# Splitting modulated rows into high and low bf16 parts: the shift taken off by GpSimd, the low part made by VectorE in one read of PSUM

## The chip, the cores and the metric

The kernel runs on one core of a Trainium2 chip. The metric is the device time of one execution in microseconds (us), smaller is better. All other times below are microseconds too, unless marked ns.

## The reference, cut to what matters

One layer of a hybrid diffusion backbone: a modulated RMSNorm feeds one combined projection (a gated convolution module and a bidirectional gated scan), an output projection follows, and then a routed mixture of 16 experts. The change is in the first part:

```python
sh1, sc1, ... = modulation(c, ada_w[l], ada_b[l])      # silu(c) @ ada_w + ada_b, split in 6
h_ctx = modulate(rmsnorm(ctx, norm1_g[l]), csh1, csc1) # h * (1 + scale) + shift
h     = modulate(rmsnorm(x, norm1_g[l]), sh1, sc1)
proj  = einsum('bnd,dc->bnc', h, w_in)                 # first use of h: columns A, B of the convolution
u     = conv(proj_A * sigmoid(proj_B), taps)
```

x has 2048 rows of 1024 channels and ctx has 256. Products of float32 operands are made from bf16 parts: each operand is a high part (its bf16 rounding) and a low part (the rest, in bf16), and three matmuls of parts stand for one product.

## The kernel before, in words

The program is a row of stages. Each stage is a block with one instruction stream per engine; all engines leave a stage before any enters the next. Two stages matter here.

**The front (`modulate_stage`, L96).** SP loads the conditioning vectors, four chunks of 512 columns of `ada_w` into `big`, then the rows: `xc` (group 0, 2 tiles of ctx), `xg1` (group 1, 4 tiles of x) and, over chunks that are used up, three more groups of 4 tiles. Two later chunks of `ada_w` (4 and 5) follow, and then the first four weight slabs of `w_in` into `wst`. TensorE multiplies each of the four chunks with the conditioning (L311, into `pm`), the result is copied (`mod_out`, L243), transposed into columns (L318) and copied again (`modc`, L263), and from it `A1` is made (L268): the factor of each channel. ScalarE squares rows for their mean squares (`square`, L207), VectorE inverts the roots (`inverse`, L248) and scales the rows (`normed`, L253).

Then comes the loop over q = 8g + k, that is 5 groups g by 8 blocks k of 128 channels, 40 steps. Called step q below:
- TensorE transposes the 2 or 4 tiles of block k into the PSUM bank `pt[q % 4]` (L331), and between the steps of the last three groups it runs the matmuls of chunks 4 and 5 (L339, two instructions each, and a bias pair, L342).
- ScalarE writes the high part `hhi` (bf16) from the bank, with factor and shift (L224); in groups 1 and 2 it also squares the rows of the group after next, from k = 4 on.
- VectorE reads the same bank again and writes the float32 value `hf` (L286); this sets the bank free for step q + 4. In groups 1 to 3 it also scales the rows of the next group, from k = 0 to 3.
- `hlo` = `hf` minus `hhi` is made by GpSimd for three steps of four and by VectorE for the fourth (L153).

VectorE copies the rows of chunks 4 and 5 out of PSUM behind groups 3 and 4 (L299); SP stores each to DRAM (L184) and waits for both stores before it leaves the stage.

**The convolution stage (`conv_stage`, L380).** ScalarE makes the high parts of weight slabs 0 to 3 (L526), VectorE their low parts (L613). TensorE takes blocks of 512 rows: each block needs two slabs (A and B columns) and 48 matmuls (L89 to L91), and there are four blocks for one pair of slabs. Block q + 2 waits until VectorE has made the gated product `u` of block q (L627). In VectorE's stream the first gated product stands behind two waits for parameters that GpSimd loads at the start of the stage: the convolution's taps and constants (L497 to L501, waited for at L618), and the gate's (L504 to L507, waited for at L621). VectorE's 124 convolution taps come next, while TensorE does the remaining blocks and other projections (jobs).

## Time and the profile before

| | us |
|---|---|
| median of 3 runs (2324.36 to 2325.8) | 2324.66 |
| the profiled execution | 2324.43 |
| its span, first to last instruction | 2322.3 |
| mean granted TensorE clock | 0.976 of full |
| end of the modulation (A1 made) | 50.95 |
| first compute of the convolution stage | 107.43 |
| its first matmul | 110.94 |

All times inside the execution count from the start of the span. The granted clock is 1.00 at 2.4 GHz and 0.50 at 1.2 GHz; a row between shows a stretch with both.

### The profile page before, as it was taken

To read this page: it belongs to the slowest core of one execution; us is meant where nothing else is said; L and a number is where in the kernel's file an instruction comes from. 1 tells how busy PE (TensorE), PEld (TensorE's weight loads), DVE (VectorE), ACT (ScalarE), POOL (GpSimd) and SP (SyncE) were. 2 spreads that over 40 slices of the span, in tenths; PEclk is the share of its full clock that TensorE was granted. 3 is DMA by queue.
4 is the path that set the end of the run, shared out by engine and by line. 5 is a ranking of instruction groups with operands and counts; after the bars stand their busy time and mean duration, and the time that the engine had idled before them with its cause. 6 is when DMAs were issued, how large, how long until landed. Compare 5 with 4: busy or idle time off the path is not lost. (4 is left out here: it accounts for less than half of the span.)

```text
span 2322.3 us, 38724 instructions
## 1 busy us (share of the span) xinstructions
PE 2188.7 (94%) x14885; PEld 1467.7 (63%) x14885; DVE 1607.5 (69%) x2235; ACT 1041.9 (45%) x1329; POOL 489.1 (21%) x535
## 2 busy tenths in 40 slices
PE   6799999999998898999976999999999999999995
PEld 3344444444878686755543777777777777777773
DVE  2839999784678787865566667666666666666666
ACT  3611002355566666644432444434444444443444
POOL 0610001012656565400003111011111111101111
PEclk9899999999999999999987999999999999999998
DMA  9341002455021120375444676676766766667776
GB/s 344 83 83 37 19 19 87 125 157 154 6 56 49 45 56 24 116 251 160 157 173 162 220 245 223 224 230 217 237 226 207 243 226 234 219 220 233 233 231 267
DMA packets 216932, 377.16 MB, mean 162 GB/s; under 512 B 38147, under 2 KB 79619, under 8 KB 216333
## 3 DMA queue, kind: packets, MB, share of 16 engines
q1 hardware_dynamic: 198702, 317.38, 40.6%
q0 software_dynamic: 16528, 56.47, 9.1%
q10 hardware_dynamic: 1616, 2.16, 0.3%
q8 instruction: 54, 0.88, 0.2%
q14 instruction: 32, 0.26, 0.0%
HBM read 313.44 MB, written 62.54 MB: 162 GB/s over the span
## 5 line engine op out<-in xcount | busy, mean ns | idle before, releaser
L89 PE MATMUL pgu<-xhi,mwhi 128*128 128x256 bf16 x2048 | 558.3, 273 | 0.0
L90 PE MATMUL pgu<-xlo,mwhi 128*128 128x256 bf16 x2048 | 558.3, 273 | 0.0
L91 PE MATMUL pgu<-xhi,mwlo 128*128 128x256 bf16 x2048 | 558.2, 273 | 0.0
L2416 DVE TENSOR_TENSOR mwlo<-mwst,mwhi 128x2048 bf16<-128x2048 f32 x187 | 426.8, 2282 | 0.0
L2313 ACT ACTIVATE mwhi<-mwst 128x2048 bf16<-128x2048 f32 x186 | 350.8, 1902 | 0.1
L2321 ACT ACTIVATE thb<-pgu 128x256 f32<-128x256 f32 x128 | 49.0, 383 | 547.2 <-PE pgu L91 547.2
L655 DVE SCALAR_TENSOR_TENSOR co<-u,taps,co 128x1984 f32<-128x1984 f32 (+22 forms) x120 | 234.1, 1951 | 3.7
L2427 DVE SCALAR_TENSOR_TENSOR thb<-thb,pgu 128x256 f32<-128x256 f32 x128 | 53.7, 420 | 258.3 <-ACT thb L2321 258.3
L90 PEld LDWEIGHTS pgu<-xlo,mwhi 128*128 128x128 bf16 x2048 | 200.4, 98 | 24.5
L89 PEld LDWEIGHTS pgu<-xhi,mwhi 128*128 128x128 bf16 x2048 | 200.4, 98 | 24.5
L2249 POOL TENSOR_TENSOR mpflag<-mpflag 1x1 f32<-1x1 f32 x46 | 37.5, 815 | 846.0 <-DVE ysb L2443 579.4
L91 PEld LDWEIGHTS pgu<-xhi,mwlo 128*128 128x128 bf16 x2048 | 200.4, 98 | 23.2
L2584 PE MATMUL pd<-mwhi,fhi 128*128 128x512 bf16 x512 | 194.1, 379 | 5.3 <-DVE ysb L2443 4.1
L2586 PE MATMUL pd<-mwhi,flo 128*128 128x512 bf16 x512 | 194.0, 379 | 0.0
L2585 PE MATMUL pd<-mwlo,fhi 128*128 128x512 bf16 x512 | 194.0, 379 | 0.0
L1497 PEld LDWEIGHTS pout<-E,KX 128*128 128x128 f32 (+2 forms) x1024 | 149.3, 180 | 43.6 <-issue 18.2
L1497 PE MATMUL pout<-E,KX 128*128 128x32 f32 (+2 forms) x1024 | 144.2, 233 | 21.0 <-DVE E L1314 12.8
L1474 PE MATMUL pj<-hhi,wst 128*128 128x512 bf16 (+1 forms) x320 | 108.3, 363 | 1.6 <-PEq L406 1.6
L2443 DVE SCALAR_TENSOR_TENSOR ysb<-pd,gate,g 128x512 f32<-128x512 f32 x64 | 47.9, 748 | 84.5 <-PE pd L2586 84.5
L1474 PE MATMUL pout<-hhi,wst 128*128 128x512 bf16 (+1 forms) x304 | 104.8, 373 | 0.0
L89 PE MATMUL pout<-hhi,whi 128*128 128x512 bf16 x256 | 97.0, 379 | 0.0
L90 PE MATMUL pout<-hlo,whi 128*128 128x512 bf16 x256 | 97.0, 379 | 0.0
(376 smaller groups left out, 4273.9 us busy)
## 6 DMA issues: line engine op xcount, KB each, us to landing
mwst<-in_w_gate SPq DMA_DIRECT2D x32, 2048.0 KB, 8.9
mwst<-in_w_up SPq DMA_DIRECT2D x32, 2048.0 KB, 7.9
mwst<-in_w_down SPq DMA_DIRECT2D x32, 2048.0 KB, 10.6
wst<-in_w_in SPq DMA_DIRECT2D x28, 512.0 KB, 6.1
big<-in_ada_w SPq DMA_DIRECT2D x5, 2048.0 KB, 14.0
s_rows<-row SPq DMA_DIRECT2D x16, 520.0 KB, 5.7
u<-in_ada_w SPq DMA_DIRECT2D x8, 1024.0 KB, 6.4
xt<-in_x SPq DMA_DIRECT2D x16, 512.0 KB, 4.3
```

Of the source, the lines that this page charges most:

```text
L89: nc.tensor.matmul(out, lh, rh, start=(first and k == 0), stop=False)
L90: nc.tensor.matmul(out, lh, rl, start=False, stop=False)
L91: ins = nc.tensor.matmul(out, ll, rh, start=False, stop=(last and k == n - 1))
L655: nc.vector.scalar_tensor_tensor(o, i, taps[:, c, k:k + 1], o, ALU.mult, ALU.add).then_inc(tap_ok, 1)
L1474: ins = nc.tensor.matmul(pj[i % 2][:, 0:n], w, x, start=(mm == 0), stop=(mm == 3 * KD - 1))
L1497: ins = nc.tensor.matmul(pat[0:keys, n * CH:(n + 1) * CH], KX[:, p, n * P:n * P + keys], E[:, p, n * CH:(n + 1) * CH], start=True, stop=True)
L2313: nc.scalar.activation(whi[:, b, ks], wst[:, b % NS, ks], ACT.Copy).then_inc(w_hi, 1)
L2416: nc.vector.tensor_tensor(wlo[:, b, ks], wst[:, b % NS, ks], whi[:, b, ks], ALU.subtract)\
L2427: nc.vector.scalar_tensor_tensor(thb[:, p], thb[:, p], 1.0, pgu[p][:, 0, :], ALU.add, ALU.mult)\
L2584: nc.tensor.matmul(pd[q % 2][:], fh, whi[:, 4 + c, k, :], start=(k == 0), stop=False)
L2585: nc.tensor.matmul(pd[q % 2][:], fh, wlo[:, 4 + c, k, :], start=False, stop=False)
L2586: last = nc.tensor.matmul(pd[q % 2][:], fl, whi[:, 4 + c, k, :], start=False, stop=(k == KD - 1))
```

## The change

The low part is taken another way. Before: hf = A1 * pt + shift, hlo = hf - hhi. Now GpSimd makes hms = hhi - shift, from SBUF alone, and VectorE makes hlo = A1 * pt - hms in one instruction, the only one in which it reads the bank. The bank becomes free with this instruction. Besides:

- The rows of group 1 are scaled ahead of the last copy of the modulation, the first two tiles of group 2 ahead of the `modc` copies, its other two tiles within group 0.
- The matmuls of chunks 4 and 5 go beside four of five of the first 20 steps of groups 2 to 4 (before: two of three of 24), and take the 128 columns of `cmix` as their stationary operand instead of the one column `sil`.
- The two copies at L299 move into groups 3 and 4 (behind k = 2 and k = 3).
- ScalarE and VectorE split weight slabs 0 and 1 within the last two groups of the front, into a buffer of their own (`wfirst`), in which the ctx rows stood before.

```diff
-        xc = m.sb("xc", [P, 2, D])
+        xc = CW_.first[:].rearrange("p a s k n -> p (a s k n)").bitcast(F32).rearrange("p (n d) -> p n d", d=D)
-        hf = m.sb("hf", [P, 4, SEG])
+        hms = m.sb("hms", [P, 4, SEG])
...
             def _(pool):
                 for q in range(NQ):
-                    if not on_dve(q):
-                        pool.wait_ge(hf_ok, q + 1)
-                        lo(nc.gpsimd, q)
+                    pool.wait_ge(hi_ok, q + 1)
+                    if q >= 4:
+                        pool.wait_ge(lo_ok, q - 3)
+                    nc.gpsimd.tensor_scalar(hms[:, q % 4, 0:width(q)], part(K["hhi"], q), shift(q), None, ALU.subtract)\
+                        .then_inc(hms_ok, 1)
...
             def _(act):
                         if k >= KD - 4 and 1 <= g < len(groups) - 2:
                             square(g + 2, k - (KD - 4))
+                        if g == len(groups) - 2 and k in (5, 7):
+                            w = (k - 5) // 2
+                            act.wait_ge(CW_.loaded[w], 16)
+                            CW_.high(nc, w, CW_.first[:, 0, w])
...
             def _(dve):
                 for n in range(NCH - 1):
                     mod_out(n)
-                inverse(0)
-                for j in range(groups[0][1]):
-                    normed(0, j)
+                for g in range(2):
+                    inverse(g)
+                    for j in range(groups[g][1]):
+                        normed(g, j)
                 mod_out(NCH - 1)
+                inverse(2)
+                normed(2, 0)
+                normed(2, 1)
                 for q in range(4):
                     dve.wait_ge(modc_ps, q + 1)
...
-                inverse(1)
-                for j in range(groups[1][1]):
-                    normed(1, j)
...
+                for g in range(len(groups)):
                     for k in range(KD):
                         q = g * KD + k
-                        dve.wait_ge(hi_ok, q + 1)
-                        if q >= 4:
-                            if on_dve(q):
-                                dve.wait_ge(lod_ok, q // 4)
-                            else:
-                                dve.wait_ge(lop_ok, pool_los(q - 4))
-                        nc.vector.tensor_scalar(hf[:, q % 4, 0:n * P], pt[q % 4][:, 0:n * P], A1[:, k, s:s + 1],
-                                                modc[:, k, s:s + 1], ALU.mult, ALU.add).then_inc(hf_ok, 1)
-                        if on_dve(q):
-                            dve.wait_ge(hf_ok, q + 1)
-                            lo(nc.vector, q)
-                        if k < 4 and 1 <= g < len(groups) - 1:
+                        dve.wait_ge(hms_ok, q + 1)
+                        nc.vector.scalar_tensor_tensor(part(K["hlo"], q), pt[q % 4][:, 0:width(q)], scale(q),
+                                                       hms[:, q % 4, 0:width(q)], ALU.mult, ALU.subtract).then_inc(lo_ok, 1)
+                        if g == 0 and k in (2, 5):
+                            normed(2, 2 + k // 5)
+                        if k < 4 and 2 <= g < len(groups) - 1:
                             if k == 0:
                                 inverse(g + 1)
                             normed(g + 1, k)
+                        if g == len(groups) - 1 and k in (0, 2):
+                            w = k // 2
+                            dve.wait_ge(CW_.hi_ok, w + 1)
+                            CW_.low(nc, w, CW_.first[:, 0, w], CW_.first[:, 1, w])
+                        if (g, k) in ((3, 2), (4, 3)):
+                            c = LATER[g - 3]
+                            dve.wait_ge(mod_ps, c + 1)
+                            dve.wait_ge(modc_ps, 4)
+                            nc.vector.tensor_copy(modrow[0:1, (c - 4) * SEG:(c - 3) * SEG], pm[c % 2][0:1, :]).then_inc(mod_sb, 1)
...
             def _(pe):
                         if q >= 4:
-                            pe.wait_ge(hf_ok, q - 3)
+                            pe.wait_ge(lo_ok, q - 3)
...
-                        if i >= 0 and i % 3 != 2:
-                            c, kk = LATER[(i - i // 3) // KD], (i - i // 3) % KD
+                        if 0 <= i < 20 and i % 5 != 4:
+                            c, kk = LATER[(i - i // 5) // KD], (i - i // 5) % KD
                             if kk == 0:
                                 pe.wait_ge(ada_in[c], 16)
-                            nc.tensor.matmul(pm[c % 2][0:1, :], K["sil"][:, kk:kk + 1], later(c)[:, kk, :], start=(kk == 0),
-                                             stop=False)
+                            nc.tensor.matmul(pm[c % 2][:], cmix[:, kk, :], later(c)[:, kk, :], start=(kk == 0), stop=False)
...
+        self.first = near.sb("wfirst", [P, 2, 2, KD, P], BF16)
+    def high(self, nc, s, out):
+        nc.scalar.activation(out, self.st[:, s % 4], ACT.Copy).then_inc(self.hi_ok, 1)
+
+    def low(self, nc, s, hi, out):
+        nc.vector.tensor_tensor(out, self.st[:, s % 4], hi, ALU.subtract).then_inc(self.lo_ok, 1)
...
-                for s in range(4):
+                for s in range(2, 4):
                     w_split(s)
```

The last hunk stands twice, in ScalarE's stream and in VectorE's. In the convolution stage slabs 0 and 1 are read from `wfirst`, and `whi` and `wlo` hold six slabs instead of eight.

## Rows read from the trace of the kernel before

**Rows 1.** The page: busy time by engine, and the chain that ended last by engine.
```profile
PE 2188.7 (94%) x14885; PEld 1467.7 (63%) x14885; DVE 1607.5 (69%) x2235; ACT 1041.9 (45%) x1329; POOL 489.1 (21%) x535
...
PE 43%; DVE 1%; issue 1%; ACT 0%; DMA 0%; POOL 0%; DVEq 0%; ACTq 0%; POOLq 0%
```

**Rows 2.** Windows: stretch, length, busy time (instructions) per engine, TensorE clock, DMA share, GB/s.
```profile
140.00:180.00 40.00, 40.00 (x187) 18.13 (x186) 23.60 (x16) 6.17 (x8) 0.76 (x1) 1.00 0.27 75
```

**Rows 3.** Who waited for whom, TensorE, 0 to 560: total, times, longest.
```profile
PE pa L89 <- DVE wlo L613: 8.7, 1, 8.7
PE pa L89 <- DVE u L627: 1.7, 1, 1.7
```

**Rows 4.** Timeline, VectorE, end of the modulation: start, length, engine, line, operation.
```profile
50.78 0.17 DVE L268 SCALAR_TENSOR_TENSOR A<-modc,n1c 128x16 f32<-128x16 f32 x1
...
51.20 2.74 DVE L253 TENSOR_SCALAR xg<-xg,rstd 128x1024 f32<-128x1024 f32 x4
53.86 1.90 DVE L286 TENSOR_SCALAR hf<-pt,A,modc 128x256 f32<-128x256 f32 x4
```

**Rows 5.** Groups by shape, whole execution: busy us, mean ns, idle before.
```profile
L1061 POOL TENSOR_SCALAR KK<-G,lh 128x512 f32<-128x512 f32 x32 | 23.6, 739 | 0.0
L2443 DVE SCALAR_TENSOR_TENSOR ysb<-pd,gate,g 128x512 f32<-128x512 f32 x64 | 47.9, 748 | 84.5 <-PE pd L2586 84.5
```

**Rows 6.** Groups by shape, 0 to 180.
```profile
L153 POOL TENSOR_TENSOR hlo<-hf,hhi 128x512 bf16<-128x512 f32 x24 | 31.6, 1340 | 12.7 <-DVE hf L286 12.6
...
L311 PEld LDWEIGHTS pm<-big,cmix 128*128 128x128 f32 x64 | 12.6, 203 | 30.1 <-issue 30.1
L613 DVE TENSOR_TENSOR wlo<-wst,whi 128x1024 bf16<-128x1024 f32 x10 | 11.8, 1219 | 3.8 <-ACT whi L526 3.8
```

**Rows 7.** Timeline, ScalarE: first step of group 1, first step of group 2.
```profile
58.41 4.19 ACT L224 ACTIVATE hhi<-pt,modc,A 128x512 bf16<-128x512 f32 x5 [1.31 <-PE pt L331]
...
69.10 0.78 ACT L224 ACTIVATE hhi<-pt,modc,A 128x512 bf16<-128x512 f32 x1
```

**Rows 8.** Timeline, TensorE, last steps of groups 2 and 4.
```profile
78.94 1.02 PE L339 MATMUL pm<-big,sil 128*1 128x512 f32 x2
...
95.61 0.66 PE L331 MATMUL pt<-ident,big 128*128 128x128 f32 x4
...
99.12 0.66 PE L331 MATMUL pt<-ident,big 128*128 128x128 f32 x4
...
101.60 0.66 PE L331 MATMUL pt<-ident,big 128*128 128x128 f32 x4
```

**Rows 9.** Timeline: VectorE's last of the front, the other engines' first after it.
```profile
104.56 0.67 DVE L299 COPY modrow<-pm 1x512 f32<-1x512 f32 x1
...
107.43 3.89 ACT L526 ACTIVATE whi<-wst 128x1024 bf16<-128x1024 f32 x4 [4.36 <-PEq L102]
...
110.94 0.61 PE L89 MATMUL pa<-hhi,whi 128*128 128x512 bf16 x1 [8.68 <-DVE wlo L613]
```

**Rows 10.** Timeline at the first stage boundary of the program.
```profile
2.13 0.29 POOL L2627 TENSOR_SCALAR_AFFINE_SELECT identb<-identb 128x128 bf16<-128x128 bf16 x1
2.73 1.28 ACT L199 ACT_TABLE_LOAD   x1 [2.73 <-PEq L2619]
```

**Rows 11.** Timeline, GpSimd, VectorE and TensorE around the first gated product.
```profile
127.02 0.78 POOL L499 DMA_DIRECT2D cb<-in_conv_bias  x1 [12.12 <-issue]
...
135.51 0.68 DVE L627 SCALAR_TENSOR_TENSOR u<-th,pa 128x512 f32<-128x512 f32 x1
...
136.25 0.39 PE L89 MATMUL pa<-hhi,whi 128*128 128x512 bf16 x1 [1.73 <-DVE u L627]
```

**Rows 12.** Windows: stretch, length, busy per engine, TensorE clock.
```profile
56.00:58.00 2.00, 1.21 (x7) 0.83 (x6) 2.00 (x5) 1.10 (x3) 1.19 (x3) 0.50 0.39 143
...
106.00:107.00 1.00, 0.00 (x0) 0.00 (x0) 0.00 (x0) 0.00 (x0) 0.00 (x0) 0.58 0.00 0
...
116.00:117.00 1.00, 1.00 (x5) 0.45 (x4) 0.00 (x0) 0.00 (x0) 0.00 (x0) 0.80 1.49 95
```

**Rows 13.** One line, all instructions of the one-input GpSimd form: ns min/median/max.
```profile
L1061 POOL TENSOR_SCALAR KK<-G,lh x40: 467/681/1607, 563.6 to 961.3; 128x512 f32<-128x512 f32 x32, 128x256 f32<-128x256 f32 x8
```

More of the change, by code:

```diff
@@ L142, in later, with part, width, shift @@
             return xg1[:].rearrange("p n d -> p (n d)").rearrange("p (k e) -> p k e", e=SEG)
-        def on_dve(q):
-            return q % 4 == 3
-        def pool_los(q):
-            return 3 * (q // 4) + min(3, q % 4 + 1)
-        def lo(engine, q):
+        def part(t, q):
             g, k = divmod(q, KD)
             t0, n = groups[g]
-            engine.tensor_tensor(K["hlo"][:, k, t0 * P:(t0 + n) * P], hf[:, q % 4, 0:n * P],
-                                 K["hhi"][:, k, t0 * P:(t0 + n) * P], ALU.subtract)\
-                .then_inc(lod_ok if on_dve(q) else lop_ok, 1)
+            return t[:, k, t0 * P:(t0 + n) * P]
+        def width(q):
+            return groups[q // KD][1] * P
+        def shift(q):
+            return modc[:, q % KD, 0:1] if q >= KD else modc[:, q % KD, 1:2]
+        def scale(q):
+            return A1[:, q % KD, 0:1] if q >= KD else A1[:, q % KD, 1:2]
         with nc.Block() as block:
@@ L218, in _ @@
                 act.wait_ge(a1_ok, 1)
-                for g, (t0, n) in enumerate(groups):
-                    s = 0 if g else 1
+                for g in range(len(groups)):
                     for k in range(KD):
@@ L223, in _ @@
                         act.wait_ge(tp_ps, q + 1)
-                        nc.scalar.activation(K["hhi"][:, k, t0 * P:(t0 + n) * P], pt[q % 4][:, 0:n * P], ACT.Identity,
-                                             bias=modc[:, k, s:s + 1], scale=A1[:, k, s:s + 1]).then_inc(hi_ok, 1)
+                        nc.scalar.activation(part(K["hhi"], q), pt[q % 4][:, 0:width(q)], ACT.Identity, bias=shift(q),
+                                             scale=scale(q)).then_inc(hi_ok, 1)
                         if k >= KD - 4 and 1 <= g < len(groups) - 2:
                             square(g + 2, k - (KD - 4))
+                        if g == len(groups) - 2 and k in (5, 7):
+                            w = (k - 5) // 2
+                            act.wait_ge(CW_.loaded[w], 16)
+                            CW_.high(nc, w, CW_.first[:, 0, w])
             @block.vector
@@ L446, in conv_stage, with high, low @@
         LATE = range(JOBS - 3, JOBS)
+        def high(w):
+            return CW_.first[:, 0, w] if w < 2 else whi[:, w - 2]
+        def low(w):
+            return CW_.first[:, 1, w] if w < 2 else wlo[:, w - 2]
         def to_store(j):
@@ L612, in w_split @@
                     w = SLAB[s][1]
-                    nc.vector.tensor_tensor(wlo[:, w], wst[:, s % 4], whi[:, w], ALU.subtract).then_inc(w_lo, 1)
-                for s in range(4):
+                    CW_.low(nc, s, high(w), low(w))
+                for s in range(2, 4):
                     w_split(s)
@@ L723, in _, with low_rows @@
                         square_sum(n + 1)
-                    def low(q):
+                    def low_rows(q):
                         dve.wait_ge(mh_ok, q + 1)
@@ L768, in job @@
                         last = triple(nc, bank[:], [
-                            (whi[:, w, k, :], wlo[:, w, k, :], K["hhi"][:, k, t0:t0 + SEG], K["hlo"][:, k, t0:t0 + SEG])
+                            (high(w)[:, k, :], low(w)[:, k, :], K["hhi"][:, k, t0:t0 + SEG], K["hlo"][:, k, t0:t0 + SEG])
                             for k in range(KD)])
@@ L781, in _ @@
                             last = triple(nc, bank[q % 2][:], [
-                                (whi[:, s, k, :], wlo[:, s, k, :], K["hhi"][:, k, t0:t0 + SEG],
+                                (high(s)[:, k, :], low(s)[:, k, :], K["hhi"][:, k, t0:t0 + SEG],
                                  K["hlo"][:, k, t0:t0 + SEG]) for k in range(KD)])
```

37 lines of the change are left out of this document (16 added, 21 removed).

## The prediction

> **What bounds the kernel now.** I read the page first. TensorE is busy 94% of the span, and of the chain that ended last TensorE is by far the largest engine [rows 1]. So what counts is where TensorE stands still. The windows show it without a gap from 140 on, at full clock, to about 540 [rows 2]: whatever comes earlier at about 136 comes earlier at the end, one to one. The list of its waits gives two places between the front and there: 8.7 us before the first matmul of the convolution stage and 1.7 us before its third block [rows 3]. The profiled execution took 2324.43, its span is 2322.3; 2.1 us lie around it. It stands 0.2 under the median, so a gain worked out in it is taken off 2324.66.
>
> **The modulation.** TensorE's first matmuls end with the fourth chunk, and A1 stands at 50.95. Then VectorE scales group 1 (2.74) and only at 53.86 reads the first bank [rows 4]: some 2.9 us in which four banks are full. The change moves these four scalings ahead, under the modulation's matmuls, where VectorE has nothing to do. Two scalings of group 2 (0.69 each, a quarter of 2.74) and a reciprocal stand ahead of the four modc copies. They end near 50.1 and the copies then run one behind the other, so A1 comes between 0 and 0.3 later: about 51.1.
>
> **Prices of the step.** GpSimd's new instruction, one SBUF input, 512 columns, is in the trace with float32 input: 739 ns [rows 5]. The same form ran from 467 ns (256 columns) to 1607 ns, median 681 [rows 13], and the two-input form that it replaces took 1340 [rows 6]. I take 0.74 and keep 0.68 to 1.6. The Trainium skill says of GpSimd (GPSIMD Engine Reference, Engine selection) that a two-input operation is about twice as slow as on VectorE while one input runs near line rate: the two rows agree. It also says (Advanced Engine Details and Errata, VectorE Performance Modes) that GpSimd and VectorE instructions in a two-port mode block each other; the scalings would be such, and by that rule the price moves up within groups 0, 2 and 3, which is a rival below. VectorE's new instruction reads a bank and an SBUF tile with a factor per partition; the nearest row is 748 ns [rows 5], about 0.70 from start to start. It replaces 5 instructions in four steps by 4. ScalarE is unchanged.
>
> **Length of one step's chain.** The bank is now held through transposes (0.53), high part (0.77), GpSimd (0.74), VectorE (0.70) and three hand-overs (about 0.1 each): 3.0, and 3.6 with TensorE at half clock. With four banks that allows a step every 0.76 to 0.9 us. Nothing in groups 1 to 4 is that quick, so the longer hold costs nothing as long as GpSimd keeps its price.
>
> **Groups 0 and 1.** In group 0 (256 columns) a round of four takes about 2.1, plus one scaling: the first bank is free at 53.2, step 8's at 55.7. TensorE at half clock, as the row of 56 to 58 has it now [rows 12], needs 0.85 for the transposes, so ScalarE starts group 1 at 56.6 instead of 58.41. Its work in group 1 (eight high parts, four squares, a root) took 10.7 [rows 7] and is not changed: group 2 starts on ScalarE at 67.1 instead of 69.10, a gain of 2.
>
> **Group 2.** The first low part ends 67.1 + 0.77 + 0.74 + 0.70 + 0.2 = 69.5. For four steps VectorE does a low part and a scaling, 1.4 each, and the transposes of steps 20 to 23 wait for these: 69.6, 71.0, 72.5, 74.0, with a matmul pair (0.95) behind each but the first. The group ends on TensorE at 75.5; it ended at 79.9 [rows 8].
>
> **Groups 3 and 4.** Now TensorE sets the pace. Three steps with two pairs took 95.61 to 99.12 [rows 8], which is 3 x 0.53 + 2 x 0.95. Group 3 has 8 steps, 6 pairs and a bias pair: 10.9, to 86.4. In group 4 are 3 steps, 3 pairs and a bias pair: 5.4, to 91.8. All pairs are done then; the rest is the chain of the last steps on VectorE. Low part 34 ends at 92.4, then come slab 1's low part (1.14; 1219 ns long [rows 6]), low part 35 (0.7), the copy (0.6), low parts 36 to 38 and, behind the wait for its transposes, 39: end at 98.2. It was 105.2 [rows 9]. The pairs now load 128 columns of weights, 203 ns each [rows 6]. These loads can lie under the transposes or stand in front of the pair; bounds are 0 and 0.2 for each of 16. I take 0.06, 1.0 in all.
>
> **The boundary.** Now the stage ends with the store of chunk 5's row: from the end of VectorE's copy at 105.23 to ScalarE's first at 107.43 are 2.2 us [rows 9]. The copy will end at 95.3, its store is back by 97.6, ahead of the last low part. A boundary without a store takes 0.3 [rows 10]. So the convolution stage starts at 98.2 + 0.3 + 1.0 = 99.5, against 107.4: **7.9 us earlier**.
>
> **The two slabs.** Before, TensorE began at 110.94, 3.5 behind the start of the stage [rows 9]. With slabs 0 and 1 ready it can begin 0.3 behind it. Their splitting costs ScalarE 2.1 in group 3 and VectorE 2.3 in group 4; the first lies under TensorE's pairs, the second is in the sum above. But the 3.2 us aren't kept. Block 2 waits for the first gated product, which stands in VectorE's stream behind GpSimd's parameter loads: GpSimd issues the next load only at 127.02 after 12.12 us, and the product starts at 135.51, TensorE at 136.25 [rows 11], 28.8 behind the start of the stage. The change leaves this chain alone. The two first blocks took 110.94 to 134.5. They will end some 24 behind the stage's start, and TensorE will wait about 5 instead of 1.73.
>
> **What the wait does to the clock.** At 106 to 107 the granted clock fell from 1.00 to 0.50, four microseconds after the last transposes (101.60), and it came back between 116 and 117, 5.4 us after matmuls had begun again [rows 8, 9, 12]. At half clock for 5.4 us TensorE loses 2.7. The wait of 1.73 left the clock alone; one of 5 is longer than those four. So I take a fall at block 2: **2.6 us lost**, and behind it TensorE has no gap in which to make it good. The Trainium skill has the same rule (TensorE: Matmul & The Clock Gate, Part 1): an array left idle returns to 1.2 GHz.
>
> **Sum.** 7.9 - 2.6 = 5.3 earlier: 2324.66 - 5.3 = 2319.4. What a measurement can tell from no change is 0.2%, 4.6 us, so faster means under 2320.0: the forecast is only just there.
>
> **Rivals.**
> - No fall of the clock at block 2 (the blocks end later than I think, or 5 us isn't enough): 7.9 earlier, 2316.8. For it: the row shows only that four idle microseconds preceded a fall. Chance 0.17.
> - The parameter chain gets shorter, and part of the slabs' 3.2 us is kept. The two slab splittings no longer run on VectorE while GpSimd writes its descriptors. Against it: most of the chain is the 12.12 us in which GpSimd does nothing visible. 8 to 11 earlier, down to 2313.7. Chance 0.10.
> - GpSimd costs 1.34, as the old form: the scalings hold it up. Then it sets the pace: 32 steps and 8 of half width, 36 x 1.34 = 48, from 52.0 to 100.2; with the last low part and the boundary the stage starts at 101.5 to 102. Gain 5.6 - 2.6 = 3: 2321.7. Chance 0.16.
> - Slower: GpSimd at the slowest seen, 1.607, in every step: 36 x 1.607 = 57.9, to 109.9, the stage starts at 111.1, 3.7 later, and the clock's 2.6 comes on top: 2331. From 1.44 us per step on (stage start 104.8) the change loses. The one row for it is a maximum of 40, whose median is 681. Chance 0.06.
> - The change does nothing to the end, since VectorE's taps bound the convolution stage and not TensorE. Against it: both start from the same first block, and TensorE has no idle time there [rows 2]. 2324.7. Chance 0.05.
>
> The forecast itself has 0.46, with a range of its own from 2317 to 2321.5: 0 to 3.2 for the weight loads, 1 for group 0's rounds, 1.7 to 3.4 for the clock. Two thirds of it lie under 2320.0. Faster: 0.31 + 0.17 + 0.10 = 0.58. Within 0.2%: 0.15 + 0.16 + 0.05 = 0.36. Slower: 0.06. The range from 2314.5 to 2322.5 leaves out the slower case, the null case and the far end of the shorter chain.
>
> **What would show it.** GpSimd's new line near 740 ns. ScalarE's first step of group 2 near 67. TensorE without waits in group 3. ScalarE's or TensorE's first of the convolution stage near 99.5, TensorE within 0.5 of the stage's start. A wait of about 5 before the third block, for the gated product, and a granted clock of 0.50 behind it. Wrong: a GpSimd line above 1.2, or banks for which TensorE waits in groups 3 and 4; the parameter chain at another length than 28.8; the clock at 1.00 at the third block.

## The result, and the profile after

The changed kernel took 2332.93 (median of 7; 2330.6 to 2334.78) against 2325.17 (2324.36 to 2326.4) for the kernel before: **0.3% slower**, ratio 1.0032 with the interval 1.0021 to 1.0044. It was run again later on another chip: 2332.38, ratio 1.0031 (1.002 to 1.0042). The forecast was 2319.4. The profiled execution took 2331.6, its span is 2328.7.

The groups by shape of the changed kernel, 0 to 180, GpSimd and then VectorE:

```profile
L195 POOL TENSOR_SCALAR hms<-hhi,modc 128x512 f32<-128x512 bf16 x32 | 52.9, 1674 | 0.0
L195 POOL TENSOR_SCALAR hms<-hhi,modc 128x256 f32<-128x256 bf16 x8 | 8.2, 1044 | 47.5 <-ACT hhi L225 47.5
...
L285 DVE SCALAR_TENSOR_TENSOR hlo<-pt,A,hms 128x512 bf16<-128x512 f32 x32 | 23.9, 748 | 19.6 <-POOL hms L195 19.6
```

The new GpSimd line costs 1674 ns, where the prediction took 740 from [rows 5]; VectorE's new line costs the 748 that was taken. The 19.6 of VectorE's idle time name the new bound. The timeline of GpSimd shows it in one row: 40 instructions from 51.90 on, 61.07 long, and no idle time inside.

```profile
51.90 61.07 POOL L195 TENSOR_SCALAR hms<-hhi,modc 128x256 f32<-128x256 bf16 x40 [47.52 <-ACT hhi L225]
115.13 7.09 POOL L511 DMA_DIRECT2D taps<-in_conv_taps  x4 [2.16 <-POOLq L102]
133.79 0.78 POOL L513 DMA_DIRECT2D cb<-in_conv_bias  x1 [11.57 <-issue]
```

Consecutive low parts on VectorE then stand 1.54 apart, each behind GpSimd:

```profile
97.07 0.75 DVE L285 SCALAR_TENSOR_TENSOR hlo<-pt,A,hms 128x512 bf16<-128x512 f32 x1 [0.79 <-POOL hms L195]
98.61 0.75 DVE L285 SCALAR_TENSOR_TENSOR hlo<-pt,A,hms 128x512 bf16<-128x512 f32 x1 [0.79 <-POOL hms L195]
...
113.01 0.75 DVE L285 SCALAR_TENSOR_TENSOR hlo<-pt,A,hms 128x512 bf16<-128x512 f32 x1 [0.79 <-POOL hms L195]
```

So a full step costs 1.54 from start to start where nothing lengthens it. 32 of these and 8 of 0.93 (half width) are 56.7; the other 4.4 of the 61.07 come in where VectorE works from SBUF beside it: ten scalings (two in group 0, four each in groups 2 and 3) and the low parts of the two early slabs, beside each of which a GpSimd instruction took 1.83. GpSimd's single instructions, and VectorE's scalings in the same stretch:

```profile
73.94 1.57 POOL L195 TENSOR_SCALAR hms<-hhi,modc 128x512 f32<-128x512 bf16 x1
75.48 2.35 POOL L195 TENSOR_SCALAR hms<-hhi,modc 128x512 f32<-128x512 bf16 x1
77.81 1.93 POOL L195 TENSOR_SCALAR hms<-hhi,modc 128x512 f32<-128x512 bf16 x1
```

```profile
74.87 1.18 DVE L258 TENSOR_SCALAR big<-big,rstd 128x1024 f32<-128x1024 f32 x1
...
76.63 0.74 DVE L258 TENSOR_SCALAR big<-big,rstd 128x1024 f32<-128x1024 f32 x1
...
78.54 0.74 DVE L258 TENSOR_SCALAR big<-big,rstd 128x1024 f32<-128x1024 f32 x1
```

The instruction of 77.81 has one scaling beside it and is 0.37 longer than the one of 73.94; that of 75.48 meets two and is 0.78 longer; the scaling at 74.87 is itself longer by 0.44. So the two engines do hold each other up, by 0.37 to 0.44 each time, about half of a scaling's 0.74, but the 1.54 is there without it.

The windows (length, busy time and instructions of PE, PEld, DVE, ACT and POOL, clock, DMA share, GB/s) show who sets the pace now. After, and below it the kernel before:

```profile
90.00:100.00 10.00, 7.41 (x34) 3.76 (x34) 6.78 (x10) 5.90 (x8) 10.00 (x6) 1.00 0.00 0
```

```profile
90.00:100.00 10.00, 9.29 (x43) 3.72 (x43) 9.93 (x15) 5.41 (x8) 7.61 (x7) 1.00 0.00 0
```

Before, TensorE and VectorE were both nearly full and GpSimd had a quarter of its time free. After, GpSimd is full and both others wait for it.

What came of that downstream, in the rows that answer to [rows 3] (TensorE's waits, 0 to 620) and [rows 9, 11] (timelines at the boundary and at the third block):

```profile
PE pt L333 <- DVE hlo L285: 14.6, 22, 1.7
...
PE pa L89 <- DVE u L641: 5.0, 1, 5.0
```

```profile
114.70 2.00 ACT L362 ACTIVATE whi<-wst 128x1024 bf16<-128x1024 f32 x2 [5.13 <-PEq L102]
115.10 0.63 PE L90 MATMUL pa<-hlo,wfirst 128*128 128x512 bf16 x1 [6.34 <-PEq L102]
...
142.28 0.68 DVE L641 SCALAR_TENSOR_TENSOR u<-th,pa 128x512 f32<-128x512 f32 x1
...
143.01 0.61 PE L89 MATMUL pa<-hhi,wfirst 128*128 128x512 bf16 x1 [4.97 <-DVE u L641]
```

The convolution stage starts at 114.70, 7.3 later than before. TensorE is with it at once, as the early slabs promise, but the third block starts 28.3 behind the stage's start (28.8 before), behind a wait of 4.97. And the clock falls in that wait:

```profile
140.00:142.00 2.00, 0.00 (x0) 0.00 (x0) 0.00 (x0) 0.00 (x0) 0.34 (x1) 0.54 0.29 2
142.00:144.00 2.00, 0.99 (x3) 0.43 (x4) 1.88 (x4) 0.00 (x0) 0.00 (x0) 0.50 0.00 0
```

The last matmul before the wait ends at 138.04; the clock falls at about 140.2 (0.54 is the mean of 140 to 142), 2.1 later. Matmuls run at 1.2 GHz from 143.01 to about 147, which costs 2. The next stage is the place to read the sum off, since TensorE has no other gap in between. Its first matmul, first before and then after:

```profile
559.82 0.27 PE L1474 MATMUL pj<-hhi,wst 128*128 128x256 bf16 x1 [1.60 <-PEq L406]
```

```profile
568.53 0.27 PE L1488 MATMUL pj<-hhi,wst 128*128 128x256 bf16 x1 [1.59 <-PEq L414]
```

That is 8.7 later: 6.8 at the third block (143.01 - 136.25) and 2 for the clock. The median moved by 7.8.

### The profile page after: what moved, and what is told of

The parts are those of the page before. It is cut to its first block and busy times, and to the rows that moved or that the text cites. A ratio compares the mean times of both kernels' runs of the same rounds, so it can differ in the third digit from the quotient of the medians.

```text
span 2328.7 us, 38579 instructions
## 1 busy us (share of the span) xinstructions
PE 2182.8 (94%) x14740; PEld 1472.0 (63%) x14885; DVE 1598.0 (69%) x2225; ACT 1042.7 (45%) x1329; POOL 516.5 (22%) x545
## 5 line engine op out<-in xcount | busy, mean ns | idle before, releaser
L2599 PE MATMUL pd<-mwlo,fhi 128*128 128x512 bf16 x497 | 188.4, 379 | 2.9 <-DVE flo L2449 1.4
L2598 PE MATMUL pd<-mwhi,fhi 128*128 128x512 bf16 x481 | 182.3, 379 | 4.2 <-DVE ysb L2457 4.1
L1488 PE MATMUL pj<-hhi,wst 128*128 128x512 bf16 (+1 forms) x306 | 101.8, 357 | 1.6 <-PEq L414 1.6
L1300 DVE TENSOR_TENSOR_SCAN B<-segm,E 128x512 f32<-128x512 f32 (+1 forms) x40 | 57.4, 1436 | 57.1 <-ACT E L1147 57.1
L549 ACT ACTIVATE jb<-pout 128x512 f32<-128x512 f32 (+1 forms) x54 | 31.5, 592 | 137.0 <-PE pout L91 119.3
```

Of the source, the lines that this page charges most:

```text
L1300: nc.vector.tensor_tensor_scan(B[:, p, way], segm[:, 0:n], E[:, p, way], 0.0, ALU.mult, ALU.add)\
L1488: ins = nc.tensor.matmul(pj[i % 2][:, 0:n], w, x, start=(mm == 0), stop=(mm == 3 * KD - 1))
L2598: nc.tensor.matmul(pd[q % 2][:], fh, whi[:, 4 + c, k, :], start=(k == 0), stop=False)
L2599: nc.tensor.matmul(pd[q % 2][:], fh, wlo[:, 4 + c, k, :], start=False, stop=False)
```

## The experiments

Each of the kernels with a time ran beside the kernel before on its chip, and the ratio is against that: the median of the kernel before was 2324.0 on the chip of "two operations", "old low part" and "no early slabs", 2325.22 on that of "before + 128 columns", "add and multiply" and the parameters on GpSimd, 2325.21 on that of the last two. The two kernels with trial instructions ran once each (2331.11 and 2332.41) and are read for the prices alone. All diffs are against the changed kernel unless said otherwise. "Next stage" is the start of TensorE's first matmul of the stage behind the convolution; "wait" is TensorE's wait before the third block, and "clock" the granted clock behind it.

| kernel | stage start | third block, wait | clock | next stage | median | ratio (interval) |
|---|---|---|---|---|---|---|
| before | 107.43 | 136.25, 1.7 | 1.00 | 559.82 | 2325.17 | |
| the change | 114.70 | 143.01, 5.0 | 0.50 | 568.53 | 2332.93 | 1.0032 (1.0021 to 1.0044) |
| two operations | 127.63 | 156.75, 6.4 | 0.50 | 582.91 | 2345.3 | 1.0095 (1.008 to 1.0111) |
| old low part | 103.82 | 132.46, 5.4 | 0.50 | 557.74 | 2321.46 | 0.9994 (0.9985 to 1.0003) |
| no early slabs | 115.18 | 143.97, 3.0 | 1.00 | 567.53 | 2331.42 | 1.0036 (1.0022 to 1.0049) |
| before + 128 columns | 106.71 | 135.73, 3.0 | 1.00 | 559.32 | 2321.73 | 0.999 (0.998 to 0.9999) |
| add and multiply | 99.56 | 128.94, 7.0 | 0.50 | 554.64 | 2322.47 | 0.9983 (0.9973 to 0.9992) |
| + parameters in the front, GpSimd | 113.48 | none | 1.00 | 559.88 | 2322.79 | 0.9989 (0.9979 to 0.9998) |
| + parameters in the front, SP | 99.24 | none | 1.00 | 545.17 | 2312.84 | 0.9942 (0.9928 to 0.9955) |
| the same, no early slabs | 102.21 | none | 1.00 | 552.94 | 2314.14 | 0.995 (0.9936 to 0.9963) |

### What makes GpSimd's instruction dear

Eight forms are tried three times each at the start of the front, where VectorE does next to nothing; the rest of the kernel is the changed one.

```diff
+                for _ in range(3):
+                    done(nc.gpsimd.tensor_scalar(o, b, col, None, ALU.subtract))
...
+                    done(nc.gpsimd.tensor_scalar(o, f, col, None, ALU.subtract))
+                    done(nc.gpsimd.tensor_scalar(o, b, 0.0, col, ALU.add, ALU.subtract))
+                    done(nc.gpsimd.tensor_scalar(o, f, -1.0, col, ALU.add, ALU.mult))
+                    done(nc.gpsimd.tensor_scalar(o, b, -1.0, col, ALU.add, ALU.mult))
+                    done(nc.gpsimd.tensor_scalar(o, b, col, None, ALU.add))
+                    done(nc.gpsimd.tensor_scalar(o, b, 1.0, None, ALU.mult))
+                    done(nc.gpsimd.tensor_tensor(o, b, f, ALU.subtract))
```

Each stands in a loop of three, as the first; b is bf16, f float32, col one value per partition. The lines are L205, L207 and so on to L219 in this order.

> The changed kernel with 24 instructions put into GpSimd's idle time at the start (some 47 us), three of each form, 512 columns, one after the other with a wait: they change nothing of the output. It prices the forms alone. The new instruction cost 1.54 to 1.56 us where 0.74 was expected. Theory A (the form with one operation and a per-partition operand is slow): bf16 and float32 input both near 1.5, the two-operation form near 0.74 with either input. Theory B (the bf16 input is slow): bf16 near 1.5 in all forms, float32 near 0.74 in all. Theory C (VectorE's scalings and bank reads hold GpSimd up): all forms near 0.74 here, where VectorE does next to nothing.

GpSimd's groups by shape, 0 to 52:

```profile
L209 POOL TENSOR_SCALAR hms<-hlo,eps 128x512 f32<-128x512 bf16 x3 | 6.0, 2005 | 0.3
L205 POOL TENSOR_SCALAR hms<-hlo,eps 128x512 f32<-128x512 bf16 x3 | 5.0, 1657 | 0.3
L207 POOL TENSOR_SCALAR hms<-hms,eps 128x512 f32<-128x512 f32 x3 | 4.7, 1567 | 0.3
...
L217 POOL TENSOR_SCALAR hms<-hlo 128x512 f32<-128x512 bf16 x3 | 4.5, 1498 | 0.3
L219 POOL TENSOR_TENSOR hms<-hlo,hms 128x512 f32<-128x512 bf16 x3 | 3.5, 1163 | 0.2
L211 POOL TENSOR_SCALAR hms<-hms,eps 128x512 f32<-128x512 f32 x3 | 2.1, 695 | 0.3
L213 POOL TENSOR_SCALAR hms<-hlo,eps 128x512 f32<-128x512 bf16 x3 | 2.1, 694 | 0.3
```

The mean of 1657 for the form of the change holds one instruction of 1836 ns (its line alone, ns min/median/max):

```profile
L205 POOL TENSOR_SCALAR hms<-hlo,eps x3: 1566/1570/1836, 5.5 to 9.1; 128x512 f32<-128x512 bf16 x3
```

It is the first, from 5.50 on, and VectorE still makes `cmix` beside it until 6.87. The other two take 1.57, the price in the kernel, with no VectorE work beside them: contention between the two engines is ruled out as the cause of the price. bf16 and float32 cost the same, in the subtraction (1.57 undisturbed, and 1567) as in the pair (694, 695): the type is ruled out too. L213 reads the same tile as L205 and costs less than half. What is left is the operations. The row of [rows 5] from which the price came (L1061) adds -1.0 and multiplies by a column; the change's instruction has one operation. A single operation is the dear case, even a multiplication by 1.0 (1498); so is add with subtract (2005), which the first theory had near 0.74.

A second set in the same place, L205 to L217 in this order, sorts the pairs.

```diff
+                    done(nc.gpsimd.tensor_scalar(o, b, col, 1.0, ALU.subtract, ALU.mult))
+                    done(nc.gpsimd.tensor_scalar(o, b, col, 1.0, ALU.add, ALU.mult))
+                    done(nc.gpsimd.tensor_scalar(o, b, 1.0, col, ALU.mult, ALU.add))
+                    done(nc.gpsimd.tensor_scalar(o, b, 1.0, col, ALU.mult, ALU.subtract))
+                    done(nc.gpsimd.tensor_scalar(o, b, 0.0, col, ALU.add, ALU.add))
+                    done(nc.gpsimd.tensor_scalar(o, b, 1.0, col, ALU.subtract, ALU.mult))
+                    done(nc.gpsimd.tensor_scalar(o, b, 0.0, 1.0, ALU.add, ALU.mult))
```

> The changed kernel with 24 more trial instructions in GpSimd's idle time at the start, three of each form, 512 columns. The first trials gave 0.69 us for add-then-multiply and 1.5 to 2.0 for a single operation or add-then-subtract, whatever the input's type. Theory A2 (a form whose second operation is a multiply is quick): subtract-then-multiply, add-then-multiply with the per-partition operand first, and both with immediates near 0.7; multiply-then-add, multiply-then-subtract and add-then-add near 2.0. Theory A3 (only add-then-multiply is quick): subtract-then-multiply near 2.0 too. Theory A4 (the per-partition operand must come second): only the last two-immediate form may be quick. A two-input subtraction of a broadcast column near 1.16 in all theories.

```profile
L205 POOL TENSOR_SCALAR hms<-hlo,eps 128x512 f32<-128x512 bf16 x3 | 6.0, 2013 | 0.3
L213 POOL TENSOR_SCALAR hms<-hlo,eps 128x512 f32<-128x512 bf16 x3 | 6.0, 2003 | 0.3
...
L209 POOL TENSOR_SCALAR hms<-hlo,eps 128x512 f32<-128x512 bf16 x3 | 2.1, 698 | 0.3
L207 POOL TENSOR_SCALAR hms<-hlo,eps 128x512 f32<-128x512 bf16 x3 | 2.1, 695 | 0.3
L217 POOL TENSOR_SCALAR hms<-hlo 128x512 f32<-128x512 bf16 x3 | 1.9, 620 | 0.3
```

Add with multiply is quick in either order (695, 698), with two immediates too (620). Each pair with a subtraction, and add with add, costs 2.0. None of the three theories came out: subtract-then-multiply is dear, against the first; multiply-then-add is quick, against the second; and the column may come first or second, against the third. A subtraction of a column in the quick form is therefore an addition of its negative.

### The price in the kernel

First the pair that turned out not to be quick, in the kernel itself:

```diff
-                    nc.gpsimd.tensor_scalar(hms[:, q % 4, 0:width(q)], part(K["hhi"], q), shift(q), None, ALU.subtract)\
+                    nc.gpsimd.tensor_scalar(hms[:, q % 4, 0:width(q)], part(K["hhi"], q), 0.0, shift(q), ALU.add, ALU.subtract)\
```

> The changed kernel with GpSimd's instruction written with two operations, add 0.0 and then subtract the shift: the same result in the form of the 0.74 us row. Theory A (form): GpSimd's instruction near 0.74, the front ends some 14 us earlier than in the changed kernel, TensorE sets the pace of groups 3 and 4, and the time is about 2319 (my forecast for the change). Theories B and C: no difference from the changed kernel, about 2333.

The instruction's median is 1997 ns, the stage starts at 127.63, and the time is 2345.3. A second operation as such is no help. The run tells something else: from the change to this kernel the stage's start moved by 12.9, the next stage by 14.4 and the median by 12.4. The front's end goes into the time about one to one, moved by the price of this one instruction.

Then the quick pair, with the negative of the shift in a column of its own:

```diff
+                nc.vector.tensor_scalar(lessc[:], modc[:, 0:KD, :], -1.0, None, ALU.mult).then_inc(less_ok, 1)
...
-                    nc.gpsimd.tensor_scalar(hms[:, q % 4, 0:width(q)], part(K["hhi"], q), shift(q), None, ALU.subtract)\
+                    nc.gpsimd.tensor_scalar(hms[:, q % 4, 0:width(q)], part(K["hhi"], q), less(q), 1.0, ALU.add, ALU.mult)\
```

> The changed kernel with GpSimd's instruction written as add minus-shift, then multiply by 1.0 (one more small VectorE instruction makes the column of minus shifts): the same result. If this form costs 0.7, the front is what my forecast took: convolution stage from about 98 to 100, wait of about 5 at the third block, time 2317 to 2319. If it costs 1.5 to 2.0, the time is that of the changed kernel or more.

```profile
L201 POOL TENSOR_SCALAR hms<-hhi,lessc 128x512 f32<-128x512 bf16 x32 | 24.6, 774 | 16.0 <-ACT hhi L231 15.7 <-DVE hlo L292 0.2
```

```profile
99.56 2.00 ACT L369 ACTIVATE whi<-wst 128x1024 bf16<-128x1024 f32 x2 [2.61 <-PEq L102]
...
128.94 0.61 PE L89 MATMUL pa<-hhi,wfirst 128*128 128x512 bf16 x1 [7.00 <-DVE u L648]
```

```profile
130.00:132.00 2.00, 2.00 (x6) 0.70 (x5) 1.75 (x3) 0.00 (x0) 0.00 (x0) 0.50 0.34 94
```

The mean of 774 holds instructions that were lengthened; the median of the line is 691 ns. The stage starts at 99.56; the prediction had 99.5. TensorE starts 0.02 behind it. The wait before the third block and the fall of the clock are there, and the next stage starts at 554.64, 5.2 earlier than before; the prediction had 5.3. The median is 2322.47, 2.75 under that of the kernel before on its chip, and the interval of the ratio spans 1.9 to 6.3 less: it is clear of none, and 5.2 lies inside it. The expected 2317 to 2319 was met by the profiled execution (2318.09), not by the median (see the last section).

### The other parts alone

The old low part (VectorE makes hf, GpSimd and VectorE subtract) with all else of the change:

```diff
-                    pool.wait_ge(hi_ok, q + 1)
...
+                    if not on_dve(q):
+                        pool.wait_ge(hf_ok, q + 1)
+                        lo(nc.gpsimd, q)
...
-                        nc.vector.scalar_tensor_tensor(part(K["hlo"], q), pt[q % 4][:, 0:width(q)], scale(q),
-                                                       hms[:, q % 4, 0:width(q)], ALU.mult, ALU.subtract).then_inc(lo_ok, 1)
+                        nc.vector.tensor_scalar(hms[:, q % 4, 0:width(q)], pt[q % 4][:, 0:width(q)], scale(q), shift(q),
+                                                ALU.mult, ALU.add).then_inc(hf_ok, 1)
```

> The changed kernel with the low part made as before (VectorE reads the bank into float32, GpSimd three of four subtractions, VectorE the fourth); scalings, matmul placing and the two early slabs stay changed. If GpSimd's instruction alone makes the change slow, the front's last low part comes at 99 to 101 instead of 113.8 and the time falls to 2318 to 2322. If the other parts share the blame, it stays above 2325.

The last low part ends at 102.78 (99 to 101 expected) and the stage starts at 103.82: the moved scalings, copies, matmuls and slabs are worth 3.6 there, and the new low part at its quick price another 4.3 (to 99.56). The median of 2321.46 lies in the expected range, but by the ratio the gain cannot be told from none (0.9994, 0.9985 to 1.0003). In the trace the third block is 3.8 earlier and the next stage 2.1: the slabs' 3 are lost in the wait of 5.4, and the clock behind it takes back 1.7.

The change without the early slabs:

```diff
-                        if g == len(groups) - 2 and k in (5, 7):
-                            w = (k - 5) // 2
-                            act.wait_ge(CW_.loaded[w], 16)
-                            CW_.high(nc, w, CW_.first[:, 0, w])
...
-                for s in range(2, 4):
+                for s in range(4):
```

> The changed kernel with slabs 0 and 1 split in the convolution stage as before. My theory: the third block waits for the parameter loads anyway, so the early slabs buy only a longer wait (5.0 instead of 1.7 us) and a fall of the clock behind it: without them the clock stays at 1.00 at the third block and the time is 2 to 3 us less than the changed kernel's, about 2330. Rival: the clock or the wait doesn't matter and the early slabs are worth up to 3 us: 2333 to 2336.

```profile
118.69 0.61 PE L89 MATMUL pa<-hhi,wfirst 128*128 128x512 bf16 x1 [9.44 <-DVE wfirst L357]
```

```profile
142.00:144.00 2.00, 0.03 (x1) 0.03 (x2) 0.92 (x4) 0.55 (x1) 0.00 (x0) 1.00 0.11 1
144.00:146.00 2.00, 2.00 (x10) 0.94 (x11) 2.00 (x3) 0.00 (x0) 0.00 (x0) 1.00 0.00 0
```

TensorE starts 3.6 later (118.69 for 115.10) and yet meets the next stage 1.0 earlier (567.53 for 568.53). Its wait before the third block is 3.0 in place of 5.0, and the clock stays at 1.00. Here the early slabs bring the third block 1.0 forward (143.01 for 143.97), half of it an earlier stage start, and cost 2 through the clock. That the clock stays at 1.00 was expected; the 2 to 3 of time were not seen: the medians (2331.42, 2332.93) do not tell the two apart.

The 128 columns alone, against the kernel before:

```diff
-                            nc.tensor.matmul(pm[c % 2][0:1, :], K["sil"][:, kk:kk + 1], later(c)[:, kk, :], start=(kk == 0),
+                            nc.tensor.matmul(pm[c % 2][:], cmix[:, kk, :], later(c)[:, kk, :], start=(kk == 0),
...
-                                nc.tensor.matmul(pm[c % 2][0:1, :], K["ones"][0:1, 0:1], adab2[0:1, c - 4, :], start=False,
+                                nc.tensor.matmul(pm[c % 2][:], K["ones"][0:1, :], adab2[0:1, c - 4, :], start=False,
```

The bias pair takes 128 columns too, as in the changed kernel.

> The kernel before with one edit: the matmuls of chunks 4 and 5 take the 128 columns of cmix as their stationary operand. In the changed kernel a step of transposes with a pair took 1.30 us where it was free to run, before 1.53. Theory: the one-column operand costs the time, so here steps with a pair come every 1.30 instead of 1.53 in groups 2 to 4, up to 16 x 0.24 = 3.8 us less in the front where TensorE sets the pace, some 2 of them in the end. Rival: the pitch comes from the order of the work and not from the operand; pitch and time stay (2324).

```profile
95.09 0.60 PE L331 MATMUL pt<-ident,big 128*128 128x128 f32 x4
95.52 1.02 PE L339 MATMUL pm<-xg,cmix 128*128 128x512 f32 x2
96.38 1.15 PE L331 MATMUL pt<-ident,big 128*128 128x128 f32 x8
```

And the kernel before:

```profile
74.84 0.66 PE L331 MATMUL pt<-ident,big 128*128 128x128 f32 x4
75.43 1.02 PE L339 MATMUL pm<-big,sil 128*1 128x512 f32 x2
76.38 1.09 PE L331 MATMUL pt<-ident,big 128*128 128x128 f32 x8
```

A step of four transposes and a pair takes 1.29 with 128 columns (95.09 to 96.38) and 1.54 with one (74.84 to 76.38). So the 128 columns do not cost up to 0.2 a pair, they save 0.25: the theory's pitch came true, and the rival's did not. But at the stage's start 0.7 is left of it, and at the next stage 0.5, not the expected 2. The interval of the ratio ends just under 1; the median is 3.5 lower than that of the kernel before, more than the 0.5 accounts for (see the last section).

### Taking the parameter chain out of the way

With the quick pair, the stage's start is won and the third block waits 7.0 for the parameters. Two kernels load them in the front, both with the edit of the quick pair. In the first GpSimd issues them:

```diff
+                pool.wait_ge(ada_in[0], 16)
+                CP_.load(nc, pool, I, GW_)
+                pool.wait_ge(less_ok, 1)
                 for q in range(NQ):
```

> As e7, and the loads of the convolution's taps and constants and of the gate's parameters issued by GpSimd in the front, behind the first chunk of ada_w, when it has nothing else to do. My theory of the third block: the wait for the first gated product (5 us) and the fall of the clock behind it (2.6) go, so it is 6 to 8 us quicker than e7. Rivals: VectorE's taps or another wait bounds the stage and it gains under 2; or the many small packets of the taps delay the front's own loads by up to 10 us.

```profile
13.58 6.97 POOL L392 DMA_DIRECT2D taps<-in_conv_taps  x4 [9.19 <-DMA big<-in_ada_w]
35.36 0.76 POOL L394 DMA_DIRECT2D cb<-in_conv_bias  x1 [14.81 <-issue]
```

The wait at the third block is gone, and the convolution stage is 8.7 shorter (446.4 from its start to the next, 455.1 with the quick pair alone). But the first high part of the front comes at 65.43, where it came at 51.49, and the front is 13.9 longer, more than the 10 that the rival had. What the front waits for lands later: the matmuls of the third chunk of `ada_w` start at 36.50, behind a wait of 4.12 for its load (31.58 and no wait with the quick pair alone), and ScalarE's first square, which waits for the ctx rows, at 46.86 (32.16). Both together give 2322.79, no better than without.

In the second SP issues them behind the weight slabs, when the front's large loads are done:

```diff
                 for s in range(4):
                     CW_.load(sp, s)
+                CP_.load(nc, sp, I, GW_)
                 for n in LATER:
```

> As e7 (GpSimd's instruction as add-then-multiply), and the parameter loads issued by SP in the front, behind the four weight slabs, when the DMA engines have no other work. The earlier placing on GpSimd took the third block's wait away (convolution stage 8.6 us shorter) but held the modulation up by 14 us. Theory: here the stage is shorter by the same 8 to 9 us and the front stays where e7 has it (stage start 99.6): 2313 to 2316, 8 to 9 below e7. Rival: the small packets hold up the stores of the chunk rows or SP's queue, and the stage starts later by up to 8 us: no gain over e7 (2322).

```profile
73.42 14.42 SPq L391 DMA_DIRECT2D taps<-in_conv_taps  x4
...
95.72 0.65 SPq L190 DMA_DIRECT2D s_modrows<-modrow  x2
```

The four loads of the taps occupy SP for 14.42. The two stores of the chunks' rows stand behind all the parameter loads in SP's stream; they are issued together at 95.72, when the second row has just been copied (95.69), so nothing is held up here, but by a hair. The stage starts at 99.24, there is no wait at the third block, the clock stays at 1.00 there, and the next stage starts at 545.17, 14.7 earlier than before and 9.5 earlier than with the quick pair alone (8 to 9 expected). **2312.84 against 2325.21, ratio 0.9942 (0.9928 to 0.9955): the version that beats both kernels.**

The same without the early slabs:

```diff
-                        if g == len(groups) - 2 and k in (5, 7):
-                            w = (k - 5) // 2
-                            act.wait_ge(CW_.loaded[w], 16)
-                            CW_.high(nc, w, CW_.first[:, 0, w])
```

> As e9, with slabs 0 and 1 split in the convolution stage. With the third block's wait gone, the early slabs should now be worth their 3.2 us, since nothing else makes TensorE wait: 3 us more than e9. Rival: the front's end gets earlier by the 2.3 us of VectorE work that the early slabs cost there, and it comes to under 1.

```profile
99.14 0.65 SPq L190 DMA_DIRECT2D s_modrows<-modrow  x2
```

```profile
102.21 2.00 ACT L362 ACTIVATE wfirst<-wst 128x1024 bf16<-128x1024 f32 x2 [4.60 <-PEq L102]
```

TensorE's first matmul of the stage comes at 105.71 behind a wait of 8.92, for 99.26, and the next stage starts 7.8 later. The 7.8 have three parts. The stage itself starts 3.0 later. Here the four loads of the taps took SP 16.10, the stores of the rows went out only at 99.14, and the stage started 2.9 behind the last low part (99.29) in place of 0.9: the rival of the experiment before, in this kernel. Then TensorE starts 3.5 behind the stage and not at once, and the half clock at the stage's start lasts 5.9 in place of 3.2, which costs 1.3. So with the parameters out of the way the early slabs are kept in full: 4.8, more than the 3.2 expected; the 3.0 are not theirs. The medians differ by 1.3 with overlapping intervals; the time does not resolve them.

The changed kernel itself, on the chip of the last two:

> The changed kernel itself, on the same chip as the others, for a comparison without the differences between chips: 2331 to 2333, 0.3% above the kernel before, with GpSimd's instructions 1.54 us apart.

It gave 2332.38, with a median of 1557 ns for GpSimd's line (1562 in the first run). So the 19.5 between it and the best version are a difference of kernels and not of chips.

## Why the prediction was wrong, point by point

**The step that failed is the price of GpSimd's instruction**, "739 ns ... The same form ran from 467 ns": that L1061 is the same form. It has the same engine, shape and number of inputs, but a pair of operations, add then multiply, where the change has a single subtraction; and the kernel's text at that line could be read. The steps take 1.54, and 1.93 beside a scaling, in place of 0.74. 1.54 lies within the bounds of 0.68 to 1.6, and beyond the break-even of 1.44 that the slower rival named. So the slower rival, given a chance of 0.06, happened near its own numbers: it had the stage's start at 111.1 and the time at 2331; measured are 114.70 and 2332.93. It was near for another reason than its own. It put the price down to the largest of 40 durations of L1061; the runs show that every instruction of the form is dear. And its step was too long (1.607 for 1.54) while it left out what made the front longer still: half-width steps of 0.93 and not half a step, and 4.4 beside VectorE's work. One of the 40 instructions of the quick pair took 1.60 as well, beside a single scaling, and the same one did in the kernel with the parameters on SP; why is open.

The rule of the Trainium skill that was weighed there (GPSIMD Engine Reference, Engine selection: one input near line rate, two inputs about twice as slow as VectorE) fits the add and multiply pair (695 ns) and is turned round for the form of the change: one input at 1570 ns is dearer than two at 1163. The measurement decides. The other rule (Advanced Engine Details and Errata, VectorE Performance Modes: the two engines block each other in a two-port mode) agrees with the traces in kind: in the changed kernel 0.37 is added where one scaling lies beside a GpSimd instruction (1.93 for 1.56). With the quick pair such instructions took 0.96 to 1.12 for 0.69 (and the one of 1.60), those beside a slab's low part 1.06 and 1.08, and four of VectorE's scalings were lengthened too, to between 0.98 and 1.19 from 0.74. In all it is 4.4 in the front of the changed kernel, and with the quick pair GpSimd has the slack to take it. The rival that took 1.34 for every step from it overrated it.

**Modulation and A1.** Forecast 0 to 0.3 later than 50.95, about 51.1; A1 stands at 50.78 (50.61 and 0.17), and at 51.04 with the quick pair. Right to 0.3.

**The length of a step's chain** ("costs nothing as long as GpSimd keeps its price"): the condition failed, and TensorE waited 22 times, 14.6 in all (9 times and 9.0 before). With the quick pair it waited 13 times, 7.2 in all, 1.5 at the most, and the stage started when forecast.

**ScalarE's start of groups 1 and 2** was to be 56.6 and 67.1 and was 58.67 and 70.47, for the same reason. With the quick pair it was 56.97 and 67.23.

**The 128 columns**, forecast at 0.06 a pair, 1.0 in all: wrong sign, 0.25 a pair are saved. In the sum of the quick version this is hidden: its pairs are done at 92.00 (forecast 91.8), with a start behind group 2 of 76.4 for 75.5; its last low part ends at 98.64 (forecast 98.2, or 99.2 with the 1.0 for the loads), and its boundary takes 0.9 and not 0.3. That 99.56 met 99.5 owes something to errors that cancel: 0.4 on the last low part and 0.6 on the boundary against the 1.0 for the loads. One sum of the prediction is off by itself: its own terms put the end of the copy at 94.8 and not 95.3 (96.00 with the quick pair); nothing hangs on it.

**The boundary and the slabs.** The store is indeed out of the way: the last low part ends at 113.76 and the stage starts at 114.70, 0.9 behind it (0.3 forecast, 2.2 before), and TensorE starts 0.4 behind the stage. That the 3.2 of the slabs are not kept is shown three times: without them the next stage starts no later (567.53 for 568.53); with the parameters out of the way they are kept (4.8 at the next stage); and the chain from stage start to first product is 27.6 in the changed kernel, 28.1 before and 28.6 with the quick pair.

**The wait of about 5 and the clock.** Right in kind: 4.97, a fall to 0.50, 2 lost (2.6 forecast). With the quick pair the wait was 7.0. 1.6 of the 2.0 are that the first two blocks ended 22.4 behind the stage's start and not 24: the half clock at the start ended after 3.0 and not after 5.4 as in [rows 12], which is 1.2 of them. The rest is the chain to the third block, 29.4 and not 28.8. The Trainium skill (TensorE: Matmul & The Clock Gate, Part 1) says that an idle array returns to 1.2 GHz; these traces agree. The prediction's guard, that four idle microseconds preceded the one fall it had seen, was not a safe measure: in the changed kernel the fall came 2.1 behind the last matmul.

**The sum.** With the price made true, the gain at the next stage is 5.2 for a forecast 5.3. In the medians 2.75 of it show, with an interval of 1.9 to 6.3, so even the mechanism's full size would have been at the edge of the 0.2%.

## What to carry to other kernels

Take the price of an instruction from a row only when engine, shape, types and the operations in the source line all agree; where they don't, the break-even price belongs into the forecast with a real chance. When a stage boundary moves earlier, look for what starts at the boundary and is long: here the parameter loads took back the early slabs and, through the clock, more; moving them to a queue with time to spare brought the next stage 9.5 forward, where the whole change with the quick pair brought 5.2. A transfer moved earlier must not land among the loads that the front waits for, nor hold up what its new queue still has to issue.

## What was not expected of the hardware

- GpSimd's one-input instruction, 512 columns: 0.69 to 0.70 for add with multiply (0.62 with two immediates), 1.49 to 1.57 for a single operation undisturbed, 2.0 for the pairs with a subtraction and for add with add; the two-input subtraction 1.16. Why a second operation can make it quicker is open.
- A matmul with one stationary column among transposes makes the step 0.25 longer than one with 128 columns. Why is open.
- GpSimd stands for 11.6 to 12.7 between the issue of the taps and its next one with nothing visible, 14.8 when the loads of the front run beside it. SP needs 14.4 for the same four issues (16.1 in the other run), and shows it as issuing.
- TensorE's clock stayed at 1.00 through waits of 1.7 and 3.0 before the third block and fell in those of 5.0, 5.4, 6.4 and 7.0. But, read in windows of 0.1, the fall comes 2.1 behind the last matmul in the waits of 5.0 and 5.4, and 4.9 and 4.6 behind it in those of 6.4 and 7.0. So a wait of 3.0 kept the clock in two runs, and nothing here shows that it always would.
- From the start of the next stage to the end, the profiled executions took 1760 to 1761.3 (eight of them; the change, 2328.7 - 568.53 = 1760.2; the quick pair 1760.6), 1762.5 (before), or 1766 (without early slabs 1766.4; parameters on SP 1766.3), though that part of the program is the same. The difference arises before the stage that follows, which starts 431.2 to 432.2 behind the next stage in the eight, 433.7 before and 437.1 in the two, and it goes with the granted clock: 0.91 in the first two stretches of 20 in the kernel before and the two, 1.00 in the eight; 0.77 in the stretch from 400 to 420 in the two, 0.91 in the others. Why the clock falls there in some executions is not shown. The quick pair's eleven times fall into 2316.4 to 2318.1 (4, mean clock 0.978 to 0.980) and 2321.6 to 2324.8 (7, mean clock 0.973 to 0.976). That is why the places in the trace resolve more than the times do.
